# Two blocks of a network on one core: where the vector engines' convolution taps, additions and modulation rows stand beside the filter stage

## The reference, cut to what matters

```python
mod = c_act @ mod_w[i] + mod_b[i]                    # 6 x 1024 modulation values
h = rmsnorm(x, norm_pre_mix[i]) * (1.0 + sc_m) + sh_m
u = h @ w1 + b1                                      # 1024 -> 2048, "pw1"
a, gt = jnp.split(u, 2, axis=-1)
u = a * jax.nn.sigmoid(gt)
u = causal_dwconv(u, dw_w) + dw_b                    # 31 taps per channel
u = jax.nn.silu(layernorm(u, ln_g, ln_b))
u = u @ w2 + b2                                      # "pw2"
...
hdn = jnp.sin(freq * (hdn @ fw2 + fb2))              # second block: the filters
h = (hdn @ fw3 + fb3) * jnp.exp(-t * deltas)         # filter taps in time, two orders
return jnp.fft.rfft(circ, axis=0)                    # and their transform
```

## Time and profile before

| what | us |
|---|---|
| median of three runs (range) | 3379.94 (3379.19 to 3384.65) |
| profiled execution, its own time | 3385.08 |
| its span, first to last instruction | 3383.3 |
| TensorE busy in the span | 3130.5 (93%) |
| VectorE busy | 1659.3 (49%) |
| ScalarE busy | 1010.8 (30%) |
| GpSimd busy | 440.7 (13%) |

### The profile page before, as it was taken

One profiled execution on the slowest core, in us unless ns is written; L12 is line 12 of the kernel. 1 busy time (PEld: TensorE's weight loads), 2 busy tenths in 40 slices (PEclk: granted clock), 3 DMA queues, 4 the chain that ended last, 5 costly groups with the idle time before them and its releaser, 6 DMA issues.

```text
span 3383.3 us, 33357 instructions
## 1 busy us (share of the span) xinstructions
PE 3130.5 (93%) x13666; PEld 2492.1 (74%) x13666; DVE 1659.3 (49%) x1850; ACT 1010.8 (30%) x1203; POOL 440.7 (13%) x183
## 2 busy tenths in 40 slices
PE   6897878889999999979999998899988999999996
PEld 1683557768888888858888877677767788888885
DVE  3777666565565554574521056477435522222225
ACT  2344445233122222223222123467223221111111
POOL 0396760000000000000210033100010000000002
PEclk8998887899999999979999999999998999999998
DMA  5113442123213331211333243442232121112112
GB/s 201 44 44 106 140 146 80 70 87 103 84 63 124 104 109 56 94 69 63 112 128 103 93 151 133 117 95 56 88 106 74 57 63 60 38 50 63 32 48 108
DMA packets 96191, 301.22 MB, mean 89 GB/s; under 512 B 11205, under 2 KB 15045, under 8 KB 95847
## 3 DMA queue, kind: packets, MB, share of 16 engines
q1 hardware_dynamic: 96040, 299.09, 27.1%
HBM read 251.34 MB, written 47.71 MB: 88 GB/s over the span
## 4 chain that ended last, share of the span: by engine, by line
PE 45%; DVE 5%; ACT 2%; issue 1%; DMA 1%; POOL 1%; SPq 0%; DVEq 0%; ACTq 0%; POOLq 0%
PE ps L710 38%; PE ps L1095 2%; PE ps L1120 1%; PE ps L756 1%; PE ps L1105 1%; DMA mainr<-sc_k 1%; DVE tmp L2266 1%; DVE tmp L2260 1%; POOL tmp L2477 1%; DVE tmp L2262 1%; ACT mainr L1562 1%; DVE cols L2316 0%; PE ps L811 0%; PE ps L797 0%; DVE mainf L1898 0%
## 5 line engine op out<-in xcount | busy, mean ns | idle before, releaser
L710 PE MATMUL ps<-mainr,wh 128*128 128x512 f32 (+1 forms) x7104 | 1947.1, 391 | 50.5 <-POOL wl L2417 11.3
L710 PEld LDWEIGHTS ps<-mainr,wh 128*128 128x128 f32 x7104 | 1338.0, 190 | 332.0 <-issue 54.8
L710 PE MATMUL ps<-mainr,wl 128*128 128x512 f32 (+1 forms) x3552 | 1132.0, 390 | 0.0
L710 PEld LDWEIGHTS ps<-mainr,wl 128*128 128x128 f32 x3552 | 672.7, 189 | 139.4
L1214 ACT CAST wh<-raw 128x1024 fp32r<-128x1024 f32 (+2 forms) x320 | 281.9, 885 | 728.1 <-PE ps L710 554.1
L1688 DVE TENSOR_TENSOR wl<-raw,wh 128x1024 fp32r<-128x1024 f32 (+2 forms) x256 | 255.2, 998 | 472.5 <-ACT wh L1214 472.4
L2417 POOL TENSOR_TENSOR wl<-raw,wh 128x1024 fp32r<-128x1024 f32 x64 | 154.3, 2419 | 454.7 <-ACT wh L1214 454.7
L1953 DVE TENSOR_TENSOR mainf<-mainf,ps 128x1024 f32<-128x1024 f32 x80 | 97.6, 1220 | 217.4 <-PE ps L710 217.0
L756 PE MATMUL ps<-mainr,wh 128*128 128x512 f32 x576 | 167.0, 414 | 40.2 <-issue 26.7
L2462 POOL TENSOR_TENSOR tmp<-tmp,mainf 128x1024 f32<-128x1024 f32 x8 | 27.5, 3438 | 1203.8 <-DVE tmp L2236 1203.8
L1992 DVE SCALAR_TENSOR_TENSOR ps<-mainf,vec,ps 128x1024 f32<-128x1024 f32 (+1 forms) x174 | 180.9, 1103 | 0.8 <-ACT ps L1403 0.7
(11 more groups left out here) (229 smaller groups left out, 2580.2 us busy)
## 6 DMA issues: line engine op xcount, KB each, us to landing
raw<-in_mod_w SPq DMA_DIRECT2D x48, 512.0 KB, 4.5
raw<-in_ada_w SPq DMA_DIRECT2D x48, 512.0 KB, 3.7
raw<-in_f_up SPq DMA_DIRECT2D x44, 512.0 KB, 4.1
raw<-in_g_up SPq DMA_DIRECT2D x44, 512.0 KB, 3.5
raw<-in_w_in SPq DMA_DIRECT2D x40, 512.0 KB, 4.1
raw<-in_pw SPq DMA_DIRECT2D x24, 512.0 KB, 3.7
sc_x<-mainf SPq DMA_DIRECT2D x24, 512.0 KB, 2.6
mainf<-sc_x SPq DMA_DIRECT2D x24, 512.0 KB, 6.2
```

The costliest lines, as they stand in the source:

```text
L710: ins = e.matmul(out, wt[:, a:b], xs[n], start=kk == 0 and t == 0, stop=kk == kt - 1 and t == 2)
```

## The change

It has five edits, all in the projection and in the filter stage. No instruction is added or taken away; only places in the engines' lists move.

- VectorE in a tap step: one tap of the convolution, where it was two (the one after `tlo` is gone).
- VectorE in a transform step: three taps, where it was two.
- TensorE's turning of a modulation row and VectorE's addition to it come after the filter step that follows the row, where they came ahead of it. ScalarE's copy of the row stays ahead.
- `DOUBLE`, the steps with two of ScalarE's products and GpSimd's additions, is (0, 2, 16, 18), where it was (9, 11, 13, 15).
- GpSimd in `pw1`: `convolve` stands inside the loop over n and adds three products after each of the two weight tiles, where it added six after both.

```diff
-DOUBLE = (9, 11, 13, 15)
+DOUBLE = (0, 2, 16, 18)
...
     turn = None                       # tensor_program
     for kind, s in OTHER:
-        if turn:
-            modulation_turn(*turn)
-            turn = None
         if kind == "f":
             filter_step(s)
+            if turn:
+                modulation_turn(*turn)
+            turn = None
         else:
             modulation(kind, s)
             turn = (kind, s)
...
                 e.tensor_tensor(k.TAPS_OF(1, step)[:, n, :], t, k.TAPS_OF(0, step)[:, n, :].bitcast(F32),
                                 ALU.subtract).then_inc(*k.to("tlo", o, step, n))
-            conv_steps(turns, 1)
             return
...
-        conv_steps(turns, 2)
+        conv_steps(turns, 3)
...
     for kind, s in OTHER:             # vector_program
-        if row:
-            modulation_add(*row)
-            row = None
         if kind == "f":
             filter_step(s)
+            if row:
+                modulation_add(*row)
+            row = None
...
     for i in range(ND):               # gpsimd_program
         for n in range(2):
             if 2 * i + n >= 3:
                 split_to(k.W["pw1", 2 * i + n] + 3)
-        convolve(POOL_TAPS[i])
+            convolve(POOL_TAPS[i] // 2)
```

## The result

The changed kernel took 3402.34 us (median of 4 runs, 3400.09 to 3402.91) beside 3380.44 of the kernel before in the same comparison: a ratio of 1.0056, 95% interval 1.0044 to 1.0068, which is +18.9 us (14.9 to 23.0); the two medians of four lie 21.9 apart. The forecast was also slower, by this wait in this place, but by 12.2 us only. The median lies above the range's 3400; the ratio, put on the 3379.94 from which the forecast was made, gives 3398.9, just inside it. Two executions of the later comparisons, one of 3680 us and one of 4561 us, were slow ones at a granted clock of 0.81 and 0.64, and the ratios leave them out.

The account below looks back on a forecast made before the run. Bound: TensorE's wait for GpSimd's lower half in the projection, VectorE in tap steps, TensorE in transform steps. 14.5 - 3.4 - 2.0 + 2.0 + 1.9 - 1.6 + 0.8 = +12.2 us, median 3392.1, range 3384 to 3400.

Parts of the forecast that it names:

- Term 1: Projection: three additions ahead of tile 4's lower half leave TensorE idle 26.6 us there; +14.5 us.
- rival (c): Projection: GpSimd falls behind for good, additions taking 3.25 us; near 3402, chance 0.04.
- rival (b): Projection: GpSimd in threes is faster, the wait of 10.35 goes; near 3364, chance 0.03.
- Term 2: Filter stage: one tap a tap step starts rows earlier, -3.4 us, plus -2.0 from the clock.
- Fewer gaps ahead of them may bring the clock back sooner: Modulation rows behind the closely waiting tap steps: 0 to -2.0 and 0 to -2.3, taken as -2.0 us.
- Term 3: Filter stage: turning a step later lengthens four row-to-row pieces by about 0.5 each, +2.0 us, plus +1.9 for the clock.
- clock part: Rows 5, 6, 8 and 9: TensorE less evenly busy, -3.4 to +3.7, taken as +1.9 us.
- Rival (a): Filter stage gives most of Term 1 back, all clock terms at their good end; about 3385, chance 0.13.
- rival (d): Clock falls in every hole: rows 5 to 9 at about 8.8, both transforms slow; near 3398, chance 0.15.
- Term 4: Last row to transforms: first transform starts earlier, step 9's bank loses 2.5; -1.6 us together, +0.8 for the clock.
- the stage's end keeps its shape: End of the filter stage: the last addition still hangs on the last transform's copy; counted at nothing.
- That execution lies 5.1 above the median: Profiled execution, 3385.08, against the median of 3379.94; used to set the median forecast at 3392.1.

Follow-up runs that it names:

- repetition: The changed kernel itself measured once more beside the kernel before: 3401.08 against 3381.53 us, ratio 1.0058.
- threes: The kernel before with only GpSimd's additions regrouped, three ahead of each lower half: 3395.86 against 3383.35 us, ratio 1.0042.
- taps: The kernel before with one tap a tap step, three a transform step and the new `DOUBLE`; turning and addition unmoved: 3380.63 us, ratio 0.9990.
- turning alone: The kernel before with only the modulation rows' turning and VectorE's addition one step later: 3392.21 us, ratio 1.0030.
- no threes: The changed kernel with GpSimd's additions as before, six behind two halves, so the other four edits alone: 3389.15 us, ratio 1.0017.
- six: The kernel before with all six additions of the second channel tile ahead of the halves of weight tiles 4 and 5: 3402.02 us, ratio 1.0060.
- pair first: The changed kernel with the halves of tiles 4 and 5 first, then six additions, groups of three afterwards: 3389.07 against 3382.42 us, ratio 1.0021.
- lead: The taps kernel with the two-half lead kept, GpSimd then alternating three additions and one half: 3372.69 against 3382.42 us, ratio 0.9972.
- early: The lead kernel with tile 6's lower half (GpSimd) and upper half (ScalarE) made ahead of the first tap: 3370.07 us, ratio 0.9964.
- the sigmoid moved: The early kernel with ScalarE's sigmoid of tile 4 ahead of the sixth product of GpSimd's taps: 3371.64 against 3381.53 us, ratio 0.9972.

## Why the prediction was right in kind and too small

**Term 1 held.** +14.5 was forecast; 14.2, 13.0 and, alone, 12.9 were measured, with the wait of 26.07 where 26.6 was said. The 1.2 between them is clock: behind the same wait tile 4 took 13.64 us in the first profile, but 12.39 in the repetition and 12.38 with the threes alone, against 10.88 at the full rate. So the 2.84 that the forecast gave to the half clock is at the upper end of what came up, and that the first profile met it is luck. No later wait on `wl` came up, so rival (c) fell, and GpSimd's first addition kept its 27.6 us behind tile 3, which ended rival (b).

**Term 2: the tap count held, its clock did not.** Row 4 began 2.4 us earlier (forecast 2.2), and no transform step became longer by its third tap. The step "Fewer gaps ahead of them may bring the clock back sooner ... I take the middle, -2.0" failed. With the taps alone, rows 4 and 7 took 9.23 and 9.52 against 9.07 and 9.29; the six rows together took 50.2 against 49.9. The three waits ahead of row 4 (6.39, 0.99 and 0.99 us) became one of 7.41, and the rows behind it were still slow. In the changed kernel rows 4 and 7 together were 0.2 and 0.7 us shorter, not 2.0.

**Term 3 was mis-sized by 2.8 us.** "Each of the four pieces from row to row gets about 0.5 longer" had the chain right: the last matmul of the step started 323.63 - 318.48 = 5.15 us behind the row's end, with 5.2 forecast. Then I gave that matmul its full-clock 0.9 us. It took 1.45, 2.07, 2.08 and 1.77 in the four places: TensorE's clock was already down behind the hole of 1.84 us, at 0.50 in the window 338.50:340.50. That is 3.7 us over four times 0.92, and with what else moved in these pieces they grew by 4.8 and 4.9, not 2.0. The hole itself was shorter than the 2.3 forecast. The term's clock part, +1.9, was too small as well: rows 5, 6, 8 and 9 took 31.55 us before, and 3.2 and 3.5 more in the two profiles of the changed kernel (2.9 more with the turning alone).

**Rival (a) fell.** The filter stage gave nothing back: it was 0.6 and 2.5 us longer, and 1.8 longer without the threes.

**What held of rival (d).** The row lengths of eleven profiles tell it best (us, rows 4 to 9):

```
addition a step later                  addition ahead of the step
changed     9.57 8.35 9.13 8.60 9.25 8.03   before   9.07 7.03 8.79 9.30 8.70 7.03
repetition  8.89 9.39 8.18 8.74 9.33 8.11   threes   9.46 8.72 7.03 8.90 7.03 8.69
no threes   9.23 8.01 8.96 8.36 9.13 7.91   six      8.85 7.03 8.71 8.94 7.03 7.03
pair first  8.38 9.14 7.92 8.67 9.28 8.07   taps     9.23 8.67 7.03 9.52 8.72 7.03
turning     9.09 8.91 8.81 8.84 8.26 8.49   lead     8.80 7.03 7.02 9.51 7.03 9.23
alone                                       early    9.35 8.72 7.03 9.38 8.73 7.03
```

Rows 4 and 7, the first and fourth of each line, have no such hole ahead of them in either column and never ran at the full-clock 7.03. Of the other 24 on the right 14 did; of the other 20 on the left none did, nor any row with the addition alone moved (7.96 to 9.92). Two more of four did with the sigmoid moved, whose addition stands ahead of the step too. So where the holes stand, the clock did not come back in time for a single row behind them. The Trainium skill ("TensorE: Matmul & The Clock Gate", "A second HAM failure mode: psum-queue depth-cycling") says that short idle spells between groups of matmuls make the clock go to and fro; for the rows the trace agrees, with the 0.75 and 0.84 above. For the transforms it agrees in one place of four in this profile, and in two in the repetition. The windows view of the changed kernel behind the holes of 1.47 and 2.35 us in the first order, then behind those of 1.85 and 2.35 in the second (PEclk is the figure ahead of the last two):

```profile
351.10:356.70 5.60, 5.59 (x24) 4.41 (x24) 0.00 (x0) 3.24 (x4) 5.52 (x3) 1.00 0.33 115
362.50:368.20 5.70, 5.70 (x25) 4.74 (x26) 2.07 (x3) 2.58 (x3) 3.64 (x3) 1.00 0.10 37
458.40:464.10 5.70, 5.68 (x25) 4.44 (x25) 0.00 (x0) 3.68 (x5) 5.38 (x3) 1.00 0.25 95
469.80:475.80 6.00, 6.00 (x19) 4.80 (x20) 0.95 (x2) 1.57 (x3) 3.09 (x2) 0.72 0.00 1
```

Over the four profiles with both taps and turning moved, all eight holes of 1.5 to 2.0 us right ahead of a first transform were followed by full clock. Of the eight of 2.35 us at the step behind it six were followed by 0.72: all four in the second order and two of four in the first. Rival (d) as I put it needed slow rows and both transforms slow. It came about in the rows and in the second order's transforms.

**Term 4 gained more than forecast, and this hid part of the miss.** From row 6's end to row 7 and from row 9's end to the mean, taken together, the changed kernel was 4.9 and 2.8 us shorter, against 2.0. The waits at steps 9 and 25 were 2.35 us each, as worked out (2.5). In the second order there was a loss too: from the first transform to the mean it took 56.7 us against 53.0, in all four profiles with both taps and turning moved, but 53.9 with the taps alone and 53.1 with the turning alone. The clock of 0.72 above is part of that, some 1.7 us, and 0.8 is VectorE's later end (the wait for `st` is 8.0 us, before 7.3); the wait of 2.35 us falls in the same stretch. The later end is a term that the forecast put at nothing ("the stage's end keeps its shape"). It is there in every profile with three taps a transform step, whatever else was moved.

**The median.** "That execution lies 5.1 above the median" was taken from three runs. Over 12 to 21 runs in each of the later comparisons the medians of the kernel before were 3381.5, 3382.4 and 3383.4, in a spread of 3376 to 3390, so the profiled 3385.08 lay 2 to 4 above. The correction was 1.6 to 3.4 us too large.

**Two sums.** Rival (c) adds 12 us to 3392.1, which is 3404 and not 3402; and -1.5 with the middle of 0 to -0.5 is -1.75, not -1.6. Neither changes what was forecast.

**Open.** Behind the filter stage, where nothing is edited, four profiles with both taps and turning moved took 2885.5 to 2886.0 us, all others 2882.6 to 2884.9. TensorE's waits there are the same for the first 75 us, so it isn't the stage's end that moves them; what does was not found. `DOUBLE` was never changed by itself. Nor was it tried to give the row a bank of its own, which would test the price of the bank directly.

## What to carry to other kernels

When a producer's list is regrouped, look at its first block: the additions that moved ahead of the first needed half were serial with TensorE one for one (26.1 us for three, 33.4 for six), and every later group was free. When a wait is moved, don't price the work behind it at full clock: here, behind a hole of 1.8 us, the next matmuls took 1.5 to 2.1 us where 0.9 was counted. And before a helper's list is reordered, read the list of the engine that feeds it, since with ScalarE's products in the way two waits were left about 2 us longer than planned.

## What was not expected of the hardware

Holes of 1.84 us on TensorE were followed at once by a granted clock of 0.75 and 0.50, while one of 1.85 ahead of a transform was not (458.42 in the trace: clock 1.00 in the 5.7 us behind it), nor any other of the eight in that place. Behind the same wait of 26.1 us tile 4 took 13.6 us in one profile and 12.4 in two others. And tile 3, ahead of every edit, began anywhere from 113.5 to 118.9 us into the span in 14 profiles, so that one profile's span says nothing to within some 3 us. The pieces between two marks are steadier, but not exact: the filter stage took 225.3 and 227.1 us in the two profiles of the changed kernel.
